# A recurrence's gate matmuls: 64-row pairs on the halves of the array in place of 128-row block-diagonal tiles, done two groups at a time

## The reference

```python
xc = causal_conv4(xr) + conv_b                      # (512, 1024)
xh = xc.reshape(1, 512, 16, 64)                     # 16 heads of 64
r = sigmoid(einsum('bshi,hio->bsho', xh, w_a) + b_a)
i = sigmoid(einsum('bshi,hio->bsho', xh, w_x) + b_x)
log_a = -8 * r * softplus(-lam)
a, b_in = exp(log_a), sqrt(-expm1(2 * log_a)) * (i * xc)
h[t] = a[t] * h[t-1] + b_in[t]                      # scan over the 512 tokens
y_c = h * gelu(gate)
```

## Time and profile before

| what | us |
|---|---|
| median of three runs | 2493.19 |
| profiled execution, its own time | 2493.3 |
| its span, first to last instruction | 2491.5 |
| TensorE busy | 2474.3 (99%) |
| ScalarE busy | 1036.4 (42%) |
| VectorE busy | 1116.7 (45%) |

### The profile page before, as it was taken

One profiled execution on the slowest core, in us unless ns is written; L12 is line 12 of the kernel. 1 busy time (PEld: TensorE's weight loads), 2 busy tenths in 40 slices (PEclk: granted clock), 3 DMA queues, 4 the chain that ended last, 5 costly groups with the idle time before them and its releaser, 6 DMA issues.

```text
span 2491.5 us, 32310 instructions
## 1 busy us (share of the span) xinstructions
PE 2474.3 (99%) x12882; PEld 2119.1 (85%) x12882; DVE 1116.7 (45%) x2339; ACT 1036.4 (42%) x2012; POOL 1133.0 (45%) x651
## 2 busy tenths in 40 slices
PE   9999999999999999999999999999999999999998
PEld 8888898888889888889888888888898888888887
DVE  7682486755415632325144545423232446434313
ACT  7552487742335322235343333333343443333323
POOL 3354355544445554444434445444544435444442
PEclk9999999999999999999999999999999999999999
DMA  5233332245332553322322222223322222222232
GB/s 213 76 102 103 94 84 75 64 161 192 138 128 85 191 198 112 104 93 77 118 76 85 85 81 88 86 86 100 110 93 85 85 77 81 89 89 81 93 97 81
DMA packets 89237, 258.79 MB, mean 104 GB/s; under 512 B 8961, under 2 KB 30209, under 8 KB 88705
## 3 DMA queue, kind: packets, MB, share of 16 engines
q1 hardware_dynamic: 89088, 256.74, 30.8%
HBM read 246.22 MB, written 2.10 MB: 100 GB/s over the span
## 4 chain that ended last, share of the span: by engine, by line
PE 91%; DVE 4%; ACT 3%; issue 1%; POOL 0%; DMA 0%; DVEq 0%; SPq 0%; POOLq 0%; ACTq 0%
PE bank L1829 89%; PE bank L1839 2%; ACT PP L2047 1%; DVE pt_lo L2350 0%; DVE Y L2350 0%; DVE nt L2350 0%; DVE C L2350 0%; DVE PP L2609 0%; ACT pt_hi L2047 0%; ACT Hhi L2047 0%; ACT blkv L2047 0%; ACT blkk L2047 0%; ACT w_hi L2047 0%; DMA XR<-in_x 0%; POOL n L2915 0%
## 5 line engine op out<-in xcount | busy, mean ns | idle before, releaser
L2910 POOL TENSOR_TENSOR w_lo<-w_raw,w_hi 128x1024 fp32r<-128x1024 f32 (+1 forms) x302 | 747.3, 2477 | 877.6 <-ACT w_hi L2047 877.4
L1829 PE MATMUL bank<-Hhi,w_hi 128*128 128x512 f32 (+1 forms) x1636 | 634.1, 388 | 0.0
L1829 PE MATMUL bank<-Hlo,w_hi 128*128 128x512 f32 (+1 forms) x1636 | 626.9, 383 | 0.1
L1829 PE MATMUL bank<-Hhi,w_lo 128*128 128x512 f32 (+1 forms) x1636 | 626.8, 383 | 0.0
L2047 ACT ACTIVATE w_hi<-w_raw 128x1024 fp32r<-128x1024 f32 (+1 forms) x318 | 326.2, 1030 | 139.2 <-DMA w_raw<-in_wa 82.5
L1829 PEld LDWEIGHTS bank<-Hhi,w_lo 128*128 128x128 f32 x1636 | 307.7, 188 | 61.5
L1829 PEld LDWEIGHTS bank<-Hlo,w_hi 128*128 128x128 f32 x1636 | 308.5, 189 | 53.4 <-POOL w_lo L2910 0.5
L1829 PEld LDWEIGHTS bank<-Hhi,w_hi 128*128 128x128 f32 x1636 | 308.2, 188 | 52.8
L2910 POOL TENSOR_TENSOR w_fifth_lo<-w_fifth_raw,w_fifth_hi 128x1024 fp32r<-128x1024 f32 x77 | 189.9, 2467 | 216.3 <-ACT w_fifth_hi L2047 216.3
L1829 PE MATMUL bank<-Hhi,w_fifth_hi 128*128 128x512 f32 x404 | 159.6, 395 | 0.0
L1829 PE MATMUL bank<-Hhi,w_fifth_lo 128*128 128x512 f32 x404 | 157.8, 390 | 0.0
(11 more groups left out here) (411 smaller groups left out, 4687.6 us busy)
## 6 DMA issues: line engine op xcount, KB each, us to landing
w_raw<-in_wb SPq DMA_DIRECT2D x169, 512.0 KB, 3.3
w_raw<-in_wa SPq DMA_DIRECT2D x139, 512.0 KB, 3.4
wm<-in_w_ada SPq DMA_DIRECT2D x48, 512.0 KB, 4.5
w_fifth_raw<-in_wb SPq DMA_DIRECT2D x42, 512.0 KB, 3.3
w_fifth_raw<-in_wa SPq DMA_DIRECT2D x35, 512.0 KB, 3.4
QQ<-Y SPq DMA_DIRECT2D x64, 128.0 KB, 2.4
wa_raw<-in_wb SPq DMA_DIRECT2D x5, 512.0 KB, 6.1
XR<-in_x SPq DMA_DIRECT2D x4, 512.0 KB, 7.6
```

What stands on the lines that cost most here:

```text
L1829: return self.e.matmul(o, lhs, rhs, start=start, stop=stop)
L2910: self.e.tensor_tensor(x.lo[:, k:k + n, :], x.raw[:, k:k + n, :], f(x.hi[:, k:k + n, :]), ALU.subtract).then_inc(*w_rest(s, k))
```

## The change

- **Weights.** One tile per group in place of two: rows 0 to 63 hold w_a and w_x of the first head side by side, rows 64 to 127 hold w_x and w_a of the second. The gates' tiles fill one slab in place of two.
- **Matmuls.** `gate_sums` issues, for each of the three parts, two matmuls of 64 rows, the lower on one bank and the upper on another. A bank then holds one gate on its partitions 0 to 63 and the other on 64 to 127.
- **Tanh.** Four instructions of 64 by 512 per group in place of two of 128 by 512; two of the four write to the other half of the partitions than they read.
- **Order.** Groups go by twos: (0, 1) behind `conv` 3, (2, 3) behind 5, (4, 5) behind 7, (6, 7) behind the first keys. The recurrence is registered behind (6, 7).
- **Banks.** The gates use (4, 5) for the first group of the two and (0, 1) for the second. From `conv` 2 on the products take turns on 6 and 7 alone; behind the gates (6, 7) the list is 6, 7, 0, 1 again.
- **Buffers.** A fourth `xs`.

```diff
         def rnn_gates(self, j):
-            for what in range(2):
-                tile = self.tile()
-                b = self.main.take()
-                names = [("gate", j, what)] + [("slab", tile.s)] * tile.ends
-                self.gate_sums(j, what, banks[b][:, :], tile, self.freed[b], names)
+            for x in range(2):
+                tile, b = self.tile(), ((4, 5), (0, 1))[x]
+                names = [("gate", j + x)] + [("slab", tile.s)] * tile.ends
+                self.gate_sums(j + x, [banks[y][:, :] for y in b], tile, [self.freed[y] for y in b], names)
                 if tile.ends:
                     self.slab_done(tile.s)
-                self.gate_tanh(j, what, banks[b][:, :])
-                self.freed[b] = [act_rnn.by("tanh", j, what)]
-                self.gated[j] = what == 1
-                yield 1
+                for y in range(2):
+                    self.gate_tanh(j + x, y, banks[b[y]])
+                    self.freed[b[y]] = [act_rnn.by("tanh", j + x, y, 1)]
+                self.gated[j + x] = True
+            yield 3
...
                 yield from self.product(self.H, ("k", gp, br), self.evac_k(gp, br))
-                if gp == 0:
-                    yield from self.rnn_gates(6 + br)
+                if gp == 0 and br == 0:
+                    yield from self.rnn_gates(6)
+                    self.t_rnn = self.later(self.recurrence())
+                    self.main.which = [6, 7, 0, 1]
...
                 self.run(self.product(H, ("conv", j), self.evac_conv(j)))
-                if j > 1:
-                    self.run(self.rnn_gates(j - 2))
+                if j == 1:
+                    self.main.which = [6, 7]
+                if j % 2 and j > 1:
+                    self.run(self.rnn_gates(j - 3))
             self.finish(t_cmp)
             self.finish(t_soft)
-            t_rnn = self.later(self.recurrence())
-
...
-            x = xs[j % 3]
+            x = xs[j % 4]
             self.wait_ge(tile.h, act_rnn.by("xs", j), bank_free, dve_rnn.by("xs", j), tile.l)
-            self.mm3(o, (tile.hi, tile.lo), (x[0][:, :], x[1][:, :]), True, True).then_inc(*sums.named(*names))
+            for n, (w, v) in enumerate(((tile.hi, x[0]), (tile.hi, x[1]), (tile.lo, x[0]))):
+                for y in range(2):
+                    ins = self.mm(o[y], w[ROWS[y], :], v[ROWS[y], :], n == 0, n == 2)
+            ins.then_inc(*sums.named(*names))
...
-            self.put((TR, TI)[what][:, j, :], o, ACT.Tanh, scale=.5, bias=half[:, 8 * what + j:8 * what + j + 1]).then_inc(
-                *act_rnn("tanh", j, what))
+            for x in range(2):
+                what = (x + y) % 2
+                self.put((TR, TI)[what][ROWS[y], j, :], o[ROWS[x], :], ACT.Tanh, scale=.5,
+                         bias=half[ROWS[x], 8 * what + j:8 * what + j + 1]).then_inc(*act_rnn("tanh", j, y, x))
...
-    wa, wx = diag(i["rnn_wa"][0]), diag(i["rnn_wx"][0])
-    gates = np.stack([wa, wx], 1).reshape(16, 128, 128)
+    wa, wx = i["rnn_wa"][0].reshape(8, 2, 64, 64), i["rnn_wx"][0].reshape(8, 2, 64, 64)
+    gates = np.concatenate([np.concatenate([wa[:, 0], wx[:, 0]], 2), np.concatenate([wx[:, 1], wa[:, 1]], 2)], 1)
```

More of the change, by code:

```diff
@@ L239, in program @@
     xs = [(at(f"xs_hi{i}", o, [128, 512], F32R), at(f"xs_lo{i}", o + 2, [128, 512], F32R))
-          for i, o in enumerate((R0 + 80, R0 + 84, R0 + 88))]
+          for i, o in enumerate((R0 + 80, R0 + 84, R0 + 88, R0 + 92))]
     Y2 = at("Y2", R0, [128, KT, 2, 512], F32R)
@@ L1784, in load_gmlp @@
         def load_gmlp(self):
-            self.wait_ge(sums.by("gate", 7, 1))
+            self.wait_ge(sums.by("gate", 7))
             self.e.dma_start(wst[:, :, :], A["wst"]).then_inc(*wst_in(0))
@@ L1894, in cmp_values, with gate_sums @@
             ins.then_inc(*cmp_sums("value"))
-        def gate_sums(self, j, what, o, tile, bank_free, names):
-            x = xs[j % 3]
+        def gate_sums(self, j, o, tile, bank_free, names):
+            x = xs[j % 4]
             self.wait_ge(tile.h, act_rnn.by("xs", j), bank_free, dve_rnn.by("xs", j), tile.l)
-            self.mm3(o, (tile.hi, tile.lo), (x[0][:, :], x[1][:, :]), True, True).then_inc(*sums.named(*names))
+            for n, (w, v) in enumerate(((tile.hi, x[0]), (tile.hi, x[1]), (tile.lo, x[0]))):
+                for y in range(2):
+                    ins = self.mm(o[y], w[ROWS[y], :], v[ROWS[y], :], n == 0, n == 2)
+            ins.then_inc(*sums.named(*names))
         def mix_sums(self, b, bank_free):
@@ L2101, in conv, with gate_tanh @@
         def conv(self, j, o, done):
-            x = xs[j % 3]
-            self.wait_ge(dve_rnn.by("conv", j, 3), sums.by("gate", j - 3, 1) if j > 2 else
+            x = xs[j % 4]
+            self.wait_ge(dve_rnn.by("conv", j, 3), sums.by("gate", j - 4) if j > 3 else
                          [act_norm.by("h", "first", KT - 1, 1), pool_norm.by("rest", "first", KT - 1, 1)])
             self.put(x[0][:, :], XC[:, j, :]).then_inc(*act_rnn("xs", j))
-        def gate_tanh(self, j, what, o):
-            self.wait_ge(sums.by("gate", j, what), ready0.by("half"), act_norm.by("h", "first", KT - 1, 1),
+        def gate_tanh(self, j, y, o):
+            self.wait_ge(sums.by("gate", j), ready0.by("half"), act_norm.by("h", "first", KT - 1, 1),
                          pool_norm.by("rest", "first", KT - 1, 1))
-            self.put((TR, TI)[what][:, j, :], o, ACT.Tanh, scale=.5, bias=half[:, 8 * what + j:8 * what + j + 1]).then_inc(
-                *act_rnn("tanh", j, what))
+            for x in range(2):
+                what = (x + y) % 2
+                self.put((TR, TI)[what][ROWS[y], j, :], o[ROWS[x], :], ACT.Tanh, scale=.5,
+                         bias=half[ROWS[x], 8 * what + j:8 * what + j + 1]).then_inc(*act_rnn("tanh", j, y, x))
         def rec_decay(self, j):
             x, r = XC[:, j, :], TR[:, j, :]
-            self.wait_ge(dve_rnn.by("start", j), act_rnn.by("tanh", j, 0), dve_soft.by("coefh"))
+            self.wait_ge(dve_rnn.by("start", j), act_rnn.by("tanh", j, 1, 1), dve_soft.by("coefh"))
             self.put(x, r, ACT.Exp, scale=coef[:, j:j + 1], bias=coef[:, j:j + 1]).then_inc(*act_rnn("decay", j))
@@ L2128, in keys_high @@
         def keys_high(self, gp, br, odd, o, done):
-            self.wait_ge(done, dve_cmp.by("value", 3), sums.by("gate", (5, 6)[br] if gp == 0 else 7, 1))
+            self.wait_ge(done, dve_cmp.by("value", 3), sums.by("gate", 5 if gp == 0 and br == 0 else 7))
             self.put(KS[gp][odd][ROWS[odd], br, :], o[ROWS[odd], :]).then_inc(*act_kqv("k", gp, br, odd))
@@ L2137, in value_split @@
             v = VS[gp][:, t + 1 - n:t + 1, :, :, :].rearrange("p t b o n -> p (t b o) n")
-            self.wait_ge(done, dve_cmp.by("value", 3), sums.by("gate", 7, 1))
+            self.wait_ge(done, dve_cmp.by("value", 3), sums.by("gate", 7))
             self.put(v[:, :, 0:64], banks[b][:, 0:256 * n].rearrange("p (x n) -> p x n", n=64)).then_inc(*act_kqv("v", gp, t))
@@ L2157, in mix_rows @@
         def mix_rows(self, b):
-            self.wait_ge(gmlp_sums.by("rows"), sums.by("gate", 7, 1))
+            self.wait_ge(gmlp_sums.by("rows"), sums.by("gate", 7))
             self.put(rw[:, :, :].rearrange("p g t -> p (g t)"), banks[b][:, :]).then_inc(*act_gmlp("rows"))
@@ L2494, in conv @@
                     *dve_rnn("conv", j, d))
-            h, l = xs[j % 3]
+            h, l = xs[j % 4]
             self.wait_ge(act_rnn.by("xs", j))
@@ L2499, in rec_start @@
         def rec_start(self, j):
-            self.wait_ge(act_rnn.by("tanh", j, 1))
+            self.wait_ge(act_rnn.by("tanh", j, 1, 1))
             self.stt(TI[:, j, :], TI[:, j, :], 1., XC[:, j, :], ALU.add, ALU.mult).then_inc(*dve_rnn("start", j))
@@ L2517, in keys_low @@
         def keys_low(self, gp, br, odd, o):
-            self.wait_ge(act_kqv.by("k", gp, br, odd), sums.by("gate", (5, 6)[br] if gp == 0 else 7, 1))
+            self.wait_ge(act_kqv.by("k", gp, br, odd), sums.by("gate", 5 if gp == 0 and br == 0 else 7))
             self.tt(KS[gp][odd][ROWS[1 - odd], br, :], o[ROWS[odd], :], f(KS[gp][odd][ROWS[odd], br, :]), ALU.subtract).then_inc(
@@ L3036, in layout @@
     seq = [tiles(kc), tiles(vc), part(xr, 0), part(xr, 1)]
-    for j in range(8):
-        seq += [part(xr, j + 2) if j < 6 else part((ks, kw)[j - 6], 0), gates[2 * j:2 * j + 2]]
+    for j in range(0, 8, 2):
+        seq += [part(xr, j + n) if j < 6 else part(ks, 0) for n in (2, 3)[:2 if j < 6 else 1]] + [gates[j:j + 2]] + ([part(kw, 0)] if j == 6 else [])
     seq += [side_by_side(np.concatenate([vs[:, 0:128], vw[:, 0:128], ng], 1)), tiles(qp[:, 0:512])]
```

9 lines of the change are left out of this document (2 added, 7 removed).

## The result

The changed kernel takes 2500.78 us (median of eight runs, 2500.01 to 2501.27) against 2493.54 for the kernel before in the same session: a ratio of 1.0028 with a 95% interval of 1.0018 to 1.0039, slower by 7.2 us. The forecast was 2497.2, no change; the range (2490 to 2501.5) holds the result, but "slower", the sign that came, had been given a chance of only 0.38. The profiled execution took 2500.1 us with a span of 2498.3, 6.8 more than before.

What follows compares the result with a forecast made beforehand. TensorE was taken to bound the kernel, unbroken from 77.35 us on. Terms: -0.45 (`kc`), -2.64 (to `conv` 7's end), +5.79 (to the values) make +2.7, with restart +4.0: 2497.2 us, counted as no change; range 2490 to 2501.5.

Steps and rivals of the forecast that it cites:

- The two waits: TensorE waiting for ScalarE's tanhs: about 1 us ahead of gates 7, 5.9 in one piece ahead of the second keys.
- the pair: Gate matmuls: two 64-row halves together take 0.235 us, within bounds of 0.227 and 0.66; 48 matmuls become 24 pairs.
- the rival of halves that don't overlap: Gate matmuls: pairs at 0.453 us give +4.4, at 0.66 +7.8; 2497.6 to 2501 us; chance 0.15.
- The estimate from the Trainium skill: Gate matmuls: 1.53 times from two row tiles makes a pair 0.295 us and the sum below 0.4 larger.
- the restart: TensorE's loss behind the 5.9 us wait at the second keys: 0 to 2.4 us, taken as 1.3.
- a sign that it is wrong: Stretch of the second keys' wait: the forecast is wrong if the granted clock falls there.
- a visit: TensorE entering and leaving the 64-row form around gates: bounds 0 to 0.35 us, 0.25 taken for each of four.
- an instruction's price goes by its columns, not its rows: ScalarE's 64-row tanhs: each takes 0.57 us, so eight of groups 4 and 5 end at 8.49.
- ScalarE is free at 3.93: Behind the end of `conv` 7: ScalarE has rounded `xs` 7 and starts the tanhs 3.93 us later, as before.
- `kc`: VectorE's last `kc`, which TensorE awaits at 77.35: 0.45 us sooner, its wait still there and longer.
- The clock falls: Rival: clock falls in the wait, slowing the second keys; restart over 2.3 us; 2498.2 to 2501.3 us; chance 0.27.
- No long wait: Rival: ScalarE is through when TensorE reaches the second keys; 2489.2 us, or 2487.7 with `kc` earlier; chance 0.13.

Runs made afterwards that it cites:

- Run 1: Changed kernel with one line moved, so that the second keys take bank 7 in place of bank 1: 2494.9 us, ratio 1.0004 to the kernel before.
- run 7: Changed kernel with two 128-row tanhs a group in place of four of 64 rows, leaving out part of the computation: 2495.16 us, ratio 1.0004 to the kernel before.
- run 10: Changed kernel with `conv` 7's four VectorE instructions ahead of `xs_lo` of 6 instead of behind it: 2499.01 us, ratio 1.002 to the kernel before.
- run 9: Changed kernel; second keys on bank 7, `conv` 7's ScalarE rounding behind tanhs of groups 4, 5, next weights' rounding ahead of recurrence's roots: 2488.55 us, ratio 0.9977.
- runs 4 and 11: Changed kernel, four 64-row tanhs a group: 4 reads both lower, then both upper halves, 2500.95 us; 11 writes each to the half it reads, 2500.74 us.
- run 2: 64-row pairs and tanhs alone, in the order of the kernel before, banks by turn from its old list: 2504.35 us, ratio 1.0043 to that kernel.
- run 8: 64-row pairs in the old order, gates on banks (4, 5) and (0, 1) in turn: 2501.09 us, ratio 1.0027 to the kernel before.
- run 5: Changed kernel with second keys on bank 7 and ScalarE's rounding of `conv` 7 behind the tanhs of groups 4 and 5: 2491.24 us, ratio 0.999.
- run 3: Order, banks and buffers of the change, with the old 128-row block-diagonal matmuls and whole tanhs: 2495.76 us, ratio 1.0006 to the kernel before.
- run 6: Changed kernel with second keys on bank 7 and ScalarE's rounding of `conv` 7 behind group 4's tanhs alone: 2493.5 us, ratio 0.9999.

## Why the prediction was nearly right, and where it was not

The change lost 7.2 us where 4.0 had been worked out and called no change: inside the range, with the likeliest sign missed.

**Right: the mechanism.** The two waits were named with their places and their releaser, about 1 us ahead of gates 7 and 5.9 ahead of the second keys for the last tanh of group 7; 1.72 and 6.88 came, with 1.69 more at gates 6. Run 1 shows that bank 1 was the cause and run 7 that ScalarE's sum was.

**Right: the pair.** 0.23 apart against 0.235 taken; the rival of halves that don't overlap is out. The estimate from the Trainium skill, TensorE: Matmul & The Clock Gate, section "Part 3: Packing small matmuls", was 0.295; the trace has full overlap for two tiles.

**Right by luck: the restart.** 1.4 came against 1.3. But 1.3 was a value between two rows, one of them with the clock up, and what came was the clock at half from about 112.6 to 122.8, which the first matmuls of the second keys paid for. The prediction had named a fall of the granted clock in this stretch as a sign that it is wrong, and that sign came.

**Mis-sized: a visit.** 0.25 was taken for entering and leaving; 1.79 - 6 x 0.23 = 0.41 came, 0.6 us over four visits.

**Failed: "an instruction's price goes by its columns, not its rows".** For one instruction that holds (0.68 either way). But the 0.57 put into the sum is a distance between starts, taken from 128-row neighbours, and it contains an overlap of 0.11 that these sixteen, each on another half than the one before, don't have. Sixteen tanhs at 0.71 are 2.2 us more. The earlier trace rows held the warning: two `KS` of 64 by 512 took 1.19, twice the 0.59 of a single one; it was read as the price of a copy. The Trainium skill, ScalarE: Activation LUTs, section "What ACT_TABLE_LOAD costs", says beside figures for 128 partitions that back-to-back instructions overlap by about 93 ns; this trace agrees at 128 rows (0.11) and has no overlap between these 64-row tanhs, of which the page does not speak.

**Failed: "ScalarE is free at 3.93".** That carried the distance of before over to a TensorE that is faster. VectorE's work is not: `conv` 6, the `vc` operations and `xs_lo` of 6 (2.03 us instead of 0.69) now crowd, and `conv` 7 begins late. ScalarE was free at 5.94, 2.0 later; run 10 takes it back.

**Mis-sized: `kc`.** It was forecast 0.45 sooner with its wait still there. The wait is gone (`xs_lo` of 3 took 0.69, not 2.09, and a `tiny` operation of `softplus` behind it 0.17, not 2.36, so that `kc` was there at 74.0, not 77.3), and `conv` 7 ended at 100.27 against 104.93, 4.7 sooner where 3.1 was forecast.

The sum closes. From the end of `conv` 7 to the values (first matmul at 126.88) lie 26.61 us: 20.94 forecast, plus 2.2, 2.0 and the restart's 1.4. Against 15.15 before that is 11.46 more; less the 4.66 won ahead of it, 6.8, the difference of the spans.

**The rivals.** "The clock falls" came, though not in the long wait but ahead of it, and its cost (1.4) stayed under the 2.3 at which it was to decide; the sign turned on ScalarE's lateness. The Trainium skill, TensorE: Matmul & The Clock Gate, section "HAM oscillation", has idle gaps put the clock to half; in this trace it fell behind two gaps of 1.69 and 1.72, before the 6.88. "No long wait" was refused by the profile, but run 9, with three further edits, has none: 5.6 us faster than before, where 4.0 to 5.5 had been worked out.

## What to carry to other kernels

When work is taken from one engine and given to another with time to spare, price the receiver's queue, with starts read from neighbours of the same shape, and list who stands behind it; idle time on average says nothing about the few microseconds that count. A wait removed in one place shows up at the next item of the same late queue (banks, then `hidk`, then the next weights), so follow it until the waits are gone. Ask of each bank or buffer taken in turn who frees it last: one line moved was worth 5.9 us here.

## What the runs showed of the hardware that was not expected

- ScalarE's 64-row tanhs that follow each other on changing halves of the partitions don't overlap (0.71 from start to start, 0.68 long; the change and runs 4 and 11), 128-row ones do (0.57, 0.68 long; run 7). A 64-row tanh behind a 128-row instruction overlapped it by 0.10 at 72.24 and by 0.09 at 92.70, and not at 106.21. Which part the rows have in this and which the halves was not tried.
- The granted clock fell behind waits of 3.21 (with 0.66 close behind), 2.54 (with 0.36) and 2.43 us (run 2), in one of 3.55 (run 7) and one of 3.94 (run 8), and at two short ones close together (1.69 and 1.72 in the change, 1.71 and 1.71 in run 1, 1.69 and 0.73 in run 8). It stayed at 1.00 behind 1.53, 2.06 (run 5), 2.47 (run 3) and 2.71 (run 6). Length alone does not order these: in run 2 pairs came right behind the 2.43 and the 2.54, in runs 3, 5 and 6 whole matmuls. Whether the pairs are the reason was not tried, and each row is one execution.
- `xs_lo`, a VectorE operation of 0.69 us, takes 2.03 to 2.09 in places; it is such a one that holds up `conv` 7:

```profile
100.42 2.03 DVE L2357 TENSOR_TENSOR xs_lo<-XC,xs_hi 128x512 fp32r<-128x512 f32 x1 [0.70 <-ACT xs_hi L2052]
...
99.50 5.20 POOL L2917 TENSOR_TENSOR w_lo<-w_raw,w_hi 128x1024 fp32r<-128x1024 f32 x2 [10.87 <-ACT w_hi L2052]
```

  It waits for GpSimd's `w_lo`. Of the 112 `xs_lo` in the 14 traces, 14 took 0.83 to 2.44; each of them had a `w_lo` beside it and ended 0.55 us behind the end of that `w_lo` (102.45 behind 101.90 here, the first of the two). The 97 with none beside them took 0.69, and so did one that met only the last 0.09 of a `w_lo`. In run 7 the `w_lo` falls elsewhere: `xs_lo` of 6 takes 0.69, and a `vc` operation of 0.22 beside the `w_lo` takes 2.31. `XC`, which reads a bank, is not stretched (2.31 beside the `w_lo` at 68.25 in the change, 2.32 with none beside it).
